# Attention units ordered by query block, with row statistics once for four heads

## The chip, the cores and the metric

One Trainium2 chip, one of its cores. The metric is the device time of one execution in microseconds (us). An execution has one launch; the time is that of the core from start to end. The engines are named TensorE (PE in the profile, its weight loads PEld), VectorE (DVE), ScalarE (ACT), GpSimd (POOL) and SyncE (SP).

## The reference

The whole model runs over 512 tokens of width 1024: two layers, each a feed-forward network, a mixer of four kinds of attention and another feed-forward network, and then a third block with a state-space part, a recurrent part and a last feed-forward network. The change is in the mixer's attention, which is computed in each of the two layers. Cut to what matters:

```python
Q_BLOCK, HEADS, HEAD_DIM = 128, 4, 64

def masked_softmax(s, mask):
    s = jnp.where(mask, s, NEG_INF)
    e = jnp.where(mask, jnp.exp(s - jnp.max(s, -1, keepdims=True)), 0.0)
    return e / jnp.maximum(jnp.sum(e, -1, keepdims=True), 1e-30)

# first mixer: per query block, causal, scale 96 ** -0.5
p = masked_softmax(s.astype(jnp.float32) * scale, k_pos[None, :] <= q_pos[:, None])
# second mixer: 31 compressed keys, selected blocks, window; three gated outputs
o = g[:, :, 0] * o_cmp + g[:, :, 1] * o_slc + g[:, :, 2] * o_win
# third mixer: an index score picks 128 keys for each query
_, idx = lax.top_k(score, n_top)
p = masked_softmax(s, (idx <= q_pos[None, :, None])[:, None])
```

With 512 tokens the selection of the second mixer takes all its blocks, and its window all past keys, so both are causal attention over all keys so far.

## The kernel before

Everything stays in the core's on-chip memory; weights stream in by DMA. The work is written in phases with a barrier between them. Each phase gives every engine its own instruction list, and semaphores order them. In each layer the mixer has the phases projections, preparation, `mixer_attention`, `mixer_stick_breaking` and output. The change is nearly all in `mixer_attention`.

`mixer_attention` first computes the index scores: 24 tiles of products with 32 rows, a ReLU on ScalarE (L1219) and a weighted sum on VectorE (L1343). The scores of the first three units are issued ahead of it. I call this the index stretch. Then it goes through 80 units. A unit is one head, one block b of 128 queries and one branch: 16 units of the first mixer, 48 of the second (compressed keys, selected, window for every head and block), 16 of the third. A unit is 128, 256, 384 or 512 keys wide by its block, a compressed one 31. The order is head by head, block within head, so that wide and narrow units take turns.

For unit u TensorE runs this loop: scores of unit u + 3 (L1163 to L1167, up to three products and one product of the identity with the mask), two dummy products of 512 columns that only keep it active (`keep_clock`, L373), the transposes of unit u's exponentials (L1178), and the values of unit u - 1 (L1189). ScalarE computes the exponentials with their row sum (L1228) of unit u + 1 and copies the transposed ones of unit u (L1238). VectorE reduces unit u + 2 to its row maximum (L1283), turns it into a bias (L1290), and finishes unit u - 1: clamp (L1296, compressed only), reciprocal (L1301), gate (L1306), product into `mix_y` (L1319 or L1323). Between them it has a round of the search for each query's 128 largest index scores: a MAX8 (L1262) and a value load and replacement (L1269). There are 48 rounds, one in each of the first 48 units: 16 over 256 columns, 16 over 384, 16 over 512. In its first eight units it also splits operands into a high and a low part (L1327).

```python
for u in range(n):
    if u + 3 < n:
        scores(u + 3)
    transposes(u)
    if u >= 1:
        values(u - 1)
```

A unit's scores lie in one of four banks, the transposes in banks 6 and 7, the values in banks 4 and 5.

Of the kernel before, what the change touches and what calls it, by code (L numbers as in the profile page):

```python
# [7 lines left out]
F32 = mybir.dt.float32  # L8
F32R = mybir.dt.float32r
BF16 = mybir.dt.bfloat16  # L10
ALU = mybir.AluOpType
# [43 lines left out]
CONST_NAMES = ["ident", "negd", "negs", "cmpm", "negl", "strict", "ntri", "nones", "ones", "sw64", "sw32", "triu"]  # L55
# [27 lines left out]
def constants():  # L83
# [6 lines left out]
    c["negs"] = (k >= q) * NEG  # L90
# [7 lines left out]
    for b in range(QB):  # L98
        m[:, b * NCMP:(b + 1) * NCMP] = (n[None, :] * 16 + 31 > (i + b * P)[:, None]) * NEG
    c["cmpm"] = m  # L100
    c["triu"] = (k <= q) * 1.0
    c["negl"] = (k > q) * NEG
# [130 lines left out]
class Core:  # L233


    def __init__(self, nc, ctx, dram, outT):
# [14 lines left out]
        self.kb = {name: self.kb_all[:, n * P:(n + 1) * P] for n, name in enumerate(CONST_NAMES[:N_BF16])}  # L251

# [116 lines left out]
def keep_clock(c, pe, bank, n):  # L369


    for _ in range(n):
        pe.matmul(c.ps[:, bank], c.kb["ident"], c.kb_all[:, 0:SEQ], start=True, stop=True, skip_group_check=True)  # L373


def setup_phase(c, following):

    nc, d = c.nc, c.dram
    with ExitStack() as ctx:
        ph = Phase(c, ctx, "setup", "x_in consts_in kb_done ones_done", following=following)  # L380
        with nc.Block() as block:
# [14 lines left out]
            @block.scalar  # L396
            def _(act):
                for u in range(2):
                    ph.split_hi(act, ph.next, 0, u, D)
                act.wait_ge(ph["consts_in"], 16)  # L400
                act.activation(c.kb_all[:], c.consts[:, 0:N_BF16 * P], ACT.Copy).then_inc(ph["kb_done"], 1)
# [392 lines left out]
class Mixer:  # L794


    def __init__(self, c):
# [18 lines left out]
        self.split = {t: (hi[t], self.hr[:, t], self.h[:, t]) for t in (IDXQ, IDXQ + 1, IDXK, NSAQ, NSAQ + 1, KSLC, KWIN, DSAQ, DSAQ + 1, DSAK)}  # L816
        self.split["kc"] = (self.kch[:], self.kcl[:], self.kc[:])
# [85 lines left out]
def mixer_preparation(c, m, l):  # L903
# [19 lines left out]
    with ExitStack() as ctx:  # L923
        ph = Phase(c, ctx, "prep", "w_in c1_in c2_in swap_done cos_done sin_done rope_done sq_done sum_done std_done rstd_done "
                   "lat_done uq_done qm_done uk_done km_done kpe_done uv_done vm_done win_done hid_done gelu_done kv_done cmp_done pad_done ukv_in")
        with nc.Block() as block:
# [58 lines left out]
            def _(act):  # L985
# [5 lines left out]
                for h in range(HEADS):  # L991
                    act.wait_ge(ph["uq_done"], h + 1)
                    act.activation(m.qm[:, h], c.ps[0:96, 4 + h], ACT.Copy).then_inc(ph["qm_done"], 1)
# [65 lines left out]
def attention_units(m, c):  # L1059

    units = []

    def part(tile, h, at):

        return [x[64 * (h % 2):64 * (h % 2) + 64, at] for x in m.split[tile][:2]]

    for h in range(HEADS):  # L1070
        for b in range(QB):
            units.append(dict(q=[m.qm[:, h, b * P:(b + 1) * P]], k=[m.km[:, h, 0:(b + 1) * P]], mask=c.kb["negd"], at=b * P, width=(b + 1) * P,
                              scale=96 ** -0.5, v=[m.vm[:, j, h * HD:(h + 1) * HD] for j in range(b + 1)], gate=None, mixer=0, h=h, b=b,
                              first=True, clamp=False))
    for h in range(HEADS):
        for b in range(QB):
            q = part(NSAQ + h // 2, h, slice(b * P, (b + 1) * P))
            units.append(dict(q=q, k=part("kc", h, slice(0, NCMP + 1)), mask=c.kb["cmpm"][:, b * NCMP:(b + 1) * NCMP], at=0, width=NCMP, scale=HD ** -0.5,
                              v=[m.vc[:]], gate=m.tok[:, b, GATE + h:GATE + h + 1], mixer=1, h=h, b=b, first=True, clamp=True))
            for br, (kt, vt) in enumerate(((KSLC, VSLC), (KWIN, VWIN))):  # L1080
                g = GATE + (br + 1) * HEADS + h
                units.append(dict(q=q, k=part(kt, h, slice(0, (b + 1) * P)), mask=c.kb["negd"], at=b * P, width=(b + 1) * P,
                                  scale=HD ** -0.5, v=[m.tok[:, j, vt:vt + HD] for j in range(b + 1)], gate=m.tok[:, b, g:g + 1],
                                  mixer=1, h=h, b=b, first=False, clamp=False))
    return units


def dsa_units(m, c, allowed):
    units = []
    for h in range(HEADS):  # L1090
        lo = 64 * (h % 2)
        for b in range(QB):
            mask = c.kb["negd"] if b == 0 else allowed[b]
            units.append(dict(q=[x[lo:lo + 64, b * P:(b + 1) * P] for x in m.split[DSAQ + h // 2][:2]],
                              k=[x[lo:lo + 64, 0:(b + 1) * P] for x in m.split[DSAK][:2]], mask=mask, at=0,
                              width=(b + 1) * P, scale=HD ** -0.5, v=[m.tok[:, j, DSAV:DSAV + HD] for j in range(b + 1)], gate=None,
                              mixer=2, h=h, b=b, first=True, clamp=False))
    return units


def mixer_attention(c, m, l):
# [17 lines left out]
    stat = c.at("att_stat", [P, 4, 8], F32, off)  # L1119
    top8 = c.at("idx_top", [P, 8], F32, off + 128)[:]  # L1120
    units = attention_units(m, c)
    n_dsa = len(units)
    units += dsa_units(m, c, allowed)
# [7 lines left out]
    with ExitStack() as ctx:  # L1131
        ph = Phase(c, ctx, "att", "hi_done lo_done rel_done relu_done acc_done scores_done max_done nmax_done exp_done sum_done rinv_done scale_done t_done "
                   "pt_done pv_done y_done top_done took_done choice_done")
        with nc.Block() as block:
            @block.tensor
            def _(pe):
# [13 lines left out]
                def scores(u):  # L1150
# [16 lines left out]
                    pe.matmul(s[:, x["at"]:x["at"] + mw], c.kb["ident"], x["mask"], start=False, stop=True).then_inc(ph["scores_done"], 1)  # L1167

                def transposes(u):
# [4 lines left out]
                    keep_clock(c, pe, 6 + u % 2, 2)  # L1174
# [6 lines left out]
                def values(u):  # L1181
                    x = units[u]
                    pe.wait_ge(ph["pt_done"], u + 1)
                    if u >= 2:

                        pe.wait_ge(ph["y_done"], u - 1)
                    w = min(P, x["width"])
                    for j, v in enumerate(x["v"]):
                        mm = pe.matmul(c.ps[:, 4 + u % 2, 0:HD], pt[0:w, u % 2, j * P:(j + 1) * P], v, start=j == 0, stop=j == len(x["v"]) - 1)  # L1189
# [18 lines left out]
            def _(act):  # L1208
                def hi(i):
                    act.activation(splits[i][0], splits[i][2], ACT.Copy).then_inc(ph["hi_done"], 1)  # L1210
# [11 lines left out]
                def exponentials(u):  # L1222
                    x = units[u]
                    act.wait_ge(ph["nmax_done"], u + 1)
                    if u >= 3:

                        act.wait_ge(ph["t_done"], u - 2)
                    act.activation(p[:, u % 3, 0:x["width"]], c.ps[:, u % 4, 0:x["width"]], ACT.Exp, scale=x["scale"],  # L1228
                                   bias=stat[:, u % 4, 1:2], accum_out=stat[:, u % 4, 2:3]).then_inc(ph["exp_done"], 1)
# [19 lines left out]
            def _(dve):  # L1249
# [29 lines left out]
                def maximum(u):  # L1279
                    x = units[u]  # L1280
                    s = u % 4
                    dve.wait_ge(ph["scores_done"], u + 1)
                    dve.reduce_max(stat[:, s, 0:1], c.ps[:, u % 4, 0:x["width"]], AXX).then_inc(ph["max_done"], 1)  # L1283

                def bias(u):
                    x = units[u]
                    s = u % 4
                    dve.wait_ge(ph["max_done"], u + 1)

                    dve.tensor_scalar(stat[:, s, 1:2], stat[:, s, 0:1], -x["scale"], 1e27, ALU.mult, ALU.min).then_inc(ph["nmax_done"], 1)  # L1290

                def clamp_sum(u):
                    dve.wait_ge(ph["exp_done"], u + 1)
                    if units[u]["clamp"]:
                        total = stat[:, u % 4, 2:3]
                        dve.tensor_scalar(total, total, 1e-30, None, ALU.max).then_inc(ph["sum_done"], 1)  # L1296

# [1138 lines left out]
```

## Time and profile before

| what | value |
|---|---|
| time, median of 3 runs | 3755.67 us (3751.5 to 3755.68) |
| time of the profiled execution | 3753.07 us |
| its span, first to last instruction | 3751.3 us |
| mean granted clock of TensorE | 0.964 of 2.4 GHz |
| TensorE busy | 3530.4 us, 94% |
| VectorE busy | 1705.3 us, 45% |
| ScalarE busy | 1437.4 us, 38% |
| units of `mixer_attention`, first layer | 614 to 769 us |
| units of `mixer_attention`, second layer | 1859 to 2015 us |

The busy time of an engine is the time in which it has an instruction in flight. Instructions overlap, so a duration is longer than the step from one start to the next; it is the steps that add up. In the timelines, instructions of one line that follow each other are merged, with their count; float32 products count twice there. The granted clock is 1.00 at 2.4 GHz and 0.50 at 1.2 GHz.

### The profile page before, as it was taken

The page shows a single profiled execution, that of the slowest core. Times are in us where ns is not written, and L with a number is a line of the kernel's source. Part 1 is how long each engine was busy: PE and PEld are TensorE (multiplying, and loading weights), DVE is VectorE, ACT ScalarE, POOL GpSimd, SP SyncE. Part 2 cuts the span into 40 slices and gives each one's busy share as a digit, 9 for nine tenths or more (in the row PEclk, how much of TensorE's full clock was granted, in tenths as well). Part 3 has the DMA queues.
Part 4 walks back from the last instruction along what each step waited for, and adds up shares of the span by engine and source line. Part 5 has one row for each costly group of instructions (what it writes and reads, how often), then busy time and mean ns, then how long its engine had stood idle before and what let it go on. Part 6 is the DMA issues. An engine that isn't in the chain of part 4 may idle for free. (4 is left out here: it accounts for less than half of the span.)

```text
span 3751.3 us, 44207 instructions
## 1 busy us (share of the span) xinstructions
PE 3530.4 (94%) x16234; PEld 2792.0 (74%) x16234; DVE 1705.3 (45%) x2929; ACT 1437.4 (38%) x2361; POOL 126.2 (3%) x92
## 2 busy tenths in 40 slices
PE   7999989989999999999899899989999899889998
PEld 5888766767887788778477688766777677768886
DVE  3333438735333433342783533345566536443332
ACT  3332424454332333232445533234554527433321
POOL 0001011001001000100200100000000000000000
PEclk9999998989999999999799999998999999999999
DMA  3332210002232223322000133311112122222231
GB/s 132 95 108 89 99 64 1 1 12 80 96 105 95 68 95 99 101 95 73 19 1 1 64 99 95 104 55 63 63 63 69 46 88 96 85 78 90 95 105 69
DMA packets 75671, 277.43 MB, mean 74 GB/s; under 512 B 12288, under 2 KB 13824, under 8 KB 74752
## 3 DMA queue, kind: packets, MB, share of 16 engines
q1 hardware_dynamic: 75520, 275.45, 22.4%
q8 instruction: 91, 1.49, 0.2%
q14 instruction: 60, 0.49, 0.0%
HBM read 273.32 MB, written 2.10 MB: 73 GB/s over the span
## 5 line engine op out<-in xcount | busy, mean ns | idle before, releaser
L318 DVE TENSOR_TENSOR wlo<-raw,whi 128x1024 fp32r<-128x1024 f32 (+2 forms) x464 | 610.0, 1315 | 1034.2 <-ACT whi L314 1034.2
L346 PE MATMUL ps<-xh,whi 128*128 128x512 f32 x2384 | 932.4, 391 | 16.3 <-DVE xl L2384 6.3
L347 PE MATMUL ps<-xl,whi 128*128 128x512 f32 x2384 | 929.0, 390 | 0.0
L348 PE MATMUL ps<-xh,wlo 128*128 128x512 f32 x2384 | 928.7, 390 | 0.0
L314 ACT ACTIVATE whi<-raw 128x1024 fp32r<-128x1024 f32 (+2 forms) x464 | 515.7, 1111 | 621.9 <-PE ps L348 613.7
L346 PEld LDWEIGHTS ps<-xh,whi 128*128 128x128 f32 x2384 | 448.4, 188 | 115.9 <-issue 22.2
L347 PEld LDWEIGHTS ps<-xl,whi 128*128 128x128 f32 x2384 | 448.6, 188 | 93.8 <-issue 0.7
L348 PEld LDWEIGHTS ps<-xh,wlo 128*128 128x128 f32 x2384 | 448.5, 188 | 93.4
L346 PE MATMUL ps<-ffn_hh,whi 128*128 128x512 f32 x880 | 346.9, 394 | 11.1 <-DVE ffn_hl L750 11.1
L347 PE MATMUL ps<-ffn_hl,whi 128*128 128x512 f32 x880 | 345.3, 392 | 0.0
L348 PE MATMUL ps<-ffn_hh,wlo 128*128 128x512 f32 x880 | 345.0, 392 | 0.0
L705 ACT ACTIVATE ffn_hh<-ffn_gate 128x512 f32 (+1 forms) x110 | 69.6, 633 | 511.8 <-DVE ffn_gate L748 511.8
L748 DVE TENSOR_TENSOR ffn_gate<-ffn_gate,ps 128x512 f32<-128x512 f32 x110 | 75.6, 688 | 282.2 <-PE ps L348 282.2
L346 PEld LDWEIGHTS ps<-ffn_hh,whi 128*128 128x128 f32 x880 | 166.9, 190 | 49.1 <-DVE ffn_hl L750 13.2
L347 PEld LDWEIGHTS ps<-ffn_hl,whi 128*128 128x128 f32 x880 | 166.4, 189 | 35.5 <-issue 1.0
L348 PEld LDWEIGHTS ps<-ffn_hh,wlo 128*128 128x128 f32 x880 | 166.8, 190 | 34.9
L1799 PE MATMUL ps<-xh,whi 128*128 128x512 f32 x384 | 160.0, 417 | 17.7 <-PEq L297 17.7
L701 ACT ACTIVATE ffn_gate<-ps 128x512 f32<-128x512 f32 x110 | 65.8, 598 | 256.3 <-PE ps L348 254.3
L1800 PE MATMUL ps<-xl,whi 128*128 128x512 f32 x384 | 152.9, 398 | 0.0
L1801 PE MATMUL ps<-xh,wlo 128*128 128x512 f32 x384 | 152.9, 398 | 0.0
L508 POOL TENSOR_TENSOR x<-x,mean_rest 128x512 f32<-128x512 f32 x48 | 77.3, 1646 | 1869.8 <-ACT mean_rest L472 1869.8
L750 DVE TENSOR_TENSOR ffn_hl<-ffn_gate,ffn_hh 128x512 f32 (+1 forms) x110 | 76.2, 693 | 98.9 <-ACT ffn_hh L705 98.9
(375 smaller groups left out, 4452.8 us busy)
## 6 DMA issues: line engine op xcount, KB each, us to landing
raw<-in_ffn_up SPq DMA_DIRECT2D x216, 512.0 KB, 3.5
raw<-in_ffn_down SPq DMA_DIRECT2D x80, 704.0 KB, 4.0
raw<-in_ssm_in SPq DMA_DIRECT2D x44, 512.0 KB, 3.5
raw<-in_mix_in SPq DMA_DIRECT2D x40, 512.0 KB, 3.5
raw<-in_lru_in SPq DMA_DIRECT2D x20, 512.0 KB, 3.6
raw<-in_mix_out SPq DMA_DIRECT2D x16, 512.0 KB, 3.6
raw<-in_ssm_out SPq DMA_DIRECT2D x16, 512.0 KB, 3.5
raw<-in_lru_out SPq DMA_DIRECT2D x8, 640.0 KB, 3.9
```

Source lines behind the costliest of these rows:

```text
L314: act.activation(self.core.whi[:, u % HALF, 0:width], self.core.raw[:, u, 0:width], ACT.Copy).then_inc(sems["hi_done"], 1)
L318: dve.tensor_tensor(self.core.wlo[:, u % HALF, 0:width], self.core.raw[:, u, 0:width], self.core.whi[:, u % HALF, 0:width].bitcast(F32), A ...
L346: pe.matmul(out, c.whi[:, h, w], xh[:, k0 + k], start=first and k == 0, stop=False)
L347: pe.matmul(out, c.whi[:, h, w], xl[:, k0 + k], start=False, stop=False)
L348: mm = pe.matmul(out, c.wlo[:, h, w], xh[:, k0 + k], start=False, stop=last and k == nk - 1)
L508: pool.tensor_tensor(c.x[:, t], c.x[:, t], c.dneg[:], ALU.add).then_inc(ph["xc_done"], 1)
L705: act.activation(hh[:, p], gate[:, u // 2], ACT.Copy).then_inc(ph["hh_done"], 1)
L748: dve.tensor_tensor(gate[:, u // 2], gate[:, u // 2], c.ps[:, u], ALU.mult).then_inc(ph["prod_done"], 1)
L750: dve.tensor_tensor(hl[:, p], gate[:, u // 2], hh[:, p].bitcast(F32), ALU.subtract).then_inc(ph["hl_done"], 1)
L1799: pe.matmul(out, c.whi[:, h, w], c.xh[:, t], start=t == 0, stop=False)
L1800: pe.matmul(out, c.whi[:, h, w], c.xl[:, t], start=False, stop=False)
L1801: mm = pe.matmul(out, c.wlo[:, h, w], c.xh[:, t], start=False, stop=t == DT - 1)
```

## The change

- **Order.** Units are grouped: for each mixer, block and branch, the four heads follow each other. First mixer blocks 0 to 3; second mixer, per block, compressed, selected and window; third mixer blocks 0 to 3. So four units of one width stand in a row, and the second mixer starts with sixteen short units (compressed, selected 128, window 128, compressed).
- **Sign.** Queries are scaled by the negative of their scale where they are copied or split anyway, and the mask is added through a negated identity. The row statistic is then the least score, and it is the bias of the exponential as it stands; the scaling instruction (L1290) falls away. For compressed units one more column, a small masked value, bounds the least score.
- **Once for four heads.** The row sums of four heads lie beside each other. Reciprocal, clamp, gate and the product into `mix_y` come once for a group, over 4 or 256 columns, in the second unit behind it. A group that adds to `mix_y` has a product into a buffer and an addition. The values of four heads share one bank.
- **Dummies.** Units narrower than 256 get three dummy products, all others two.
- The constants for the masks of two other phases change their sign too.

The core of the diff:

```diff
+    for b in range(QB):
+        own, past = slice(b * P, (b + 1) * P), slice(0, (b + 1) * P)
+        q = lambda h: part(NSAQ + h // 2, h, own)
+        group(1, b, q, lambda h: part("kc", h, slice(0, NCMP + 1)), c.kb["cmpm"][:, b * (NCMP + 1):(b + 1) * (NCMP + 1)], 0, NCMP,
+              lambda h: [m.vc[:]], gate=m.tok[:, b, GATE:GATE + HEADS], least=NCMP + 1)
+        for br, (kt, vt) in enumerate(((KSLC, VSLC), (KWIN, VWIN))):
+            g = GATE + (br + 1) * HEADS
+            group(1, b, q, lambda h: part(kt, h, past), c.kb["negd"], b * P, (b + 1) * P,
+                  lambda h: [m.tok[:, j, vt:vt + HD] for j in range(b + 1)], gate=m.tok[:, b, g:g + HEADS], first=False)
...
-                    pe.matmul(s[:, x["at"]:x["at"] + mw], c.kb["ident"], x["mask"], start=False, stop=True).then_inc(ph["scores_done"], 1)
+                    pe.matmul(s[:, x["at"]:x["at"] + mw], c.kb["nident"], x["mask"], start=False, stop=True).then_inc(ph["scores_done"], 1)
...
-                    keep_clock(c, pe, 6 + u % 2, 2)
+                    keep_clock(c, pe, 6 + u % 2, 3 if x["width"] < 2 * P else 2)
...
-                    if u >= 2:
-
-                        pe.wait_ge(ph["y_done"], u - 1)
+                    if u % HEADS == 0 and u >= 2 * HEADS:
+
+                        pe.wait_ge(ph["y_done"], u // HEADS - 1)
...
-                    act.wait_ge(ph["nmax_done"], u + 1)
+                    act.wait_ge(ph["least_done"], u + 1)
+                    if u % HEADS == 0 and u >= 2 * HEADS:
+
+                        act.wait_ge(ph["rinv_done"], u // HEADS - 1)
...
+                def minimum(u):
                     x = units[u]
                     dve.wait_ge(ph["scores_done"], u + 1)
+                    if u >= 4:
+
+                        dve.wait_ge(ph["exp_done"], u - 3)
+                    dve.tensor_reduce(least[:, u % 4:u % 4 + 1], c.ps[:, u % 4, 0:x["least"]], AXX, ALU.min).then_inc(ph["least_done"], 1)
+
+                def finish(n):
+
+                    g = groups[n]
+                    tot, inv = total[:, n % 2], inverse[:, n % 2]
+                    dve.wait_ge(ph["exp_done"], HEADS * (n + 1))
+                    if g["clamp"]:
+                        dve.tensor_scalar(tot, tot, 1e-30, None, ALU.max).then_inc(ph["sum_done"], 1)
+                        dve.wait_ge(ph["sum_done"], sum(y["clamp"] for y in groups[:n + 1]))
+                    dve.reciprocal(inv, tot).then_inc(ph["rinv_done"], 1)
+                    dve.wait_ge(ph["rinv_done"], n + 1)
+                    if g["gate"] is not None:
+                        dve.tensor_tensor(inv, inv, g["gate"], ALU.mult).then_inc(ph["scale_done"], 1)
+                        dve.wait_ge(ph["scale_done"], sum(y["gate"] is not None for y in groups[:n + 1]))
+                    dve.wait_ge(ph["pv_done"], HEADS * (n + 1))
...
+                    if g["first"]:
+                        dve.tensor_tensor(out.rearrange(heads, d=HD), src, factor, ALU.mult).then_inc(ph["y_done"], 1)
                     else:
+                        dve.tensor_tensor(part[:].rearrange(heads, d=HD), src, factor, ALU.mult).then_inc(ph["part_done"], 1)
+                        dve.wait_ge(ph["part_done"], sum(not y["first"] for y in groups[:n + 1]))
+                        dve.wait_ge(ph["y_done"], n)
+                        dve.tensor_tensor(out, out, part[:], ALU.add).then_inc(ph["y_done"], 1)
...
                 for u in range(n):
                     if u + 2 < n:
+                        minimum(u + 2)
                     largest()
+                    if u % HEADS == 1 and u > HEADS:
+                        finish(u // HEADS - 1)
                     take()
                     if u < len(splits) - n_index:
                         lo(n_index + u)
+                    allow()
+                finish(len(groups) - 1)
```

## Rows read from the trace of the kernel before

**Rows 1.** Windows: stretch, length, busy (PE, PEld, DVE, ACT, POOL), clock, DMA.
```profile
593.00:612.80 19.80, 19.09 (x81) 16.75 (x81) 14.63 (x30) 12.22 (x27) 0.00 (x0) 0.52 0.00 1
614.00:618.00 4.00, 4.00 (x16) 2.29 (x14) 3.87 (x15) 2.94 (x11) 0.00 (x0) 0.52 0.00 0
645.04:667.16 22.12, 22.12 (x146) 16.31 (x146) 21.31 (x100) 10.48 (x36) 0.00 (x0) 1.00 0.00 1
667.16:689.46 22.30, 22.30 (x146) 16.25 (x146) 21.76 (x94) 9.68 (x34) 0.00 (x0) 1.00 0.01 1
689.46:713.97 24.51, 23.31 (x146) 16.20 (x146) 22.83 (x99) 10.03 (x38) 0.00 (x0) 1.00 0.00 1
1935.14:1959.66 24.52, 23.32 (x147) 16.20 (x147) 22.83 (x99) 10.04 (x38) 0.00 (x0) 1.00 0.00 1
```

**Rows 2.** Timeline of TensorE, third mixer: start, duration (us), instruction.
```profile
744.59 0.50 PE L1163 MATMUL ps<-index_hi,mix_h_split 64*128 64x512 f32 x1
...
745.70 0.59 PE L373 MATMUL ps<-consts_bf 128*128 128x512 bf16 x2
746.13 0.27 PE L1178 MATMUL ps<-consts_sb,att_p 128*128 128x128 f32 x1
746.24 1.00 PE L1189 MATMUL ps<-mix_tok_sb,att_pt 128*128 128x64 f32 x8
747.18 0.33 PE L1163 MATMUL ps<-index_hi,mix_h_split 64*128 64x128 f32 x1
```

**Rows 3.** Timeline of TensorE, short units of the second mixer.
```profile
669.67 0.27 PE L1178 MATMUL ps<-consts_sb,att_p 128*128 128x128 f32 x1
669.88 0.43 PE L1189 MATMUL ps<-cmp_v,att_pt 31*128 31x64 f32 x2
670.24 0.38 PE L1163 MATMUL ps<-mix_h_split 64*128 64x256 f32 x1
...
670.85 0.59 PE L373 MATMUL ps<-consts_bf 128*128 128x512 bf16 x2
671.29 0.27 PE L1178 MATMUL ps<-consts_sb,att_p 128*128 128x128 f32 x1
671.39 0.33 PE L1189 MATMUL ps<-mix_tok_sb,att_pt 128*128 128x64 f32 x2
671.66 0.28 PE L1163 MATMUL ps<-cmp_k_hi,mix_h_split 64*128 64x32 f32 x1
...
672.13 0.59 PE L373 MATMUL ps<-consts_bf 128*128 128x512 bf16 x2
```

**Rows 4.** Timeline of VectorE, one unit beside a search round of 512 columns.
```profile
682.89 0.68 DVE L1283 TENSOR_REDUCE att_stat<-ps 128x1 f32<-128x512 f32 x1
683.49 0.68 DVE L1262 MAX8 idx_top<-idx_score 128x8 f32<-128x512 f32 x1
...
684.21 0.09 DVE L1269 MATCH_VALUE_LOAD idx_score<-idx_top,idx_score 128x8 f32 x1
684.28 0.68 DVE L1269 MATCH_REPLACE8 idx_score<-idx_top,idx_score 128x512 f32<-128x512 f32 x1
684.88 0.15 DVE L1306 TENSOR_TENSOR att_stat<-att_stat,mix_tok_sb 128x1 f32<-128x1 f32 x1
...
685.26 0.68 DVE L1283 TENSOR_REDUCE att_stat<-ps 128x1 f32<-128x512 f32 x1
```

**Rows 5.** Statistics by tile: count, then shortest/median/longest duration in ns.
```profile
L1283 DVE TENSOR_REDUCE att_stat<-ps x160: 178/414/686, 595.7 to 2010.1; 128x1 f32<-128x128 f32 x32, 128x1 f32<-128x256 f32 x32, 128x1 f32<-128x384 f32 x32, 128x1 f32<-128x512 f32 x32
...
L1262 DVE MAX8 idx_top<-idx_score x96: 415/551/686, 614.9 to 1951.9; 128x8 f32<-128x256 f32 x32, 128x8 f32<-128x384 f32 x32, 128x8 f32<-128x512 f32 x32
```

**Rows 6.** Timeline of TensorE, scores ahead of the index stretch.
```profile
593.11 0.46 PE L1163 MATMUL ps<-mla_k,mla_q 96*128 96x128 f32 x2 [1.18 <-PEq L297]
...
593.47 0.65 PE L1163 MATMUL ps<-mla_k,mla_q 96*128 96x256 f32 x2
...
594.02 1.59 PE L1163 MATMUL ps<-mla_k,mla_q 96*128 96x384 f32 x2
```

More of the change, by code:

```diff
@@ L1056, in mixer_preparation, with attention_groups @@
         ph.end()
-def attention_units(m, c):
-    units = []
+def attention_groups(m, c, allowed):
+    groups = []
     def part(tile, h, at):
         return [x[64 * (h % 2):64 * (h % 2) + 64, at] for x in m.split[tile][:2]]
[L1070 to L1085, printed above, removed]
@@ L1088, in dsa_units, with group @@
[L1088 to L1098, printed above, removed]
+    def group(mixer, b, q, k, mask, at, width, v, gate=None, first=True, least=None):
+        units = [dict(q=q(h), k=k(h), mask=mask, at=at, width=width, least=least or width, v=v(h), h=h) for h in range(HEADS)]
+        groups.append(dict(units=units, mixer=mixer, b=b, gate=gate, first=first, clamp=least is not None))
@@ L1101, in mixer_attention @@
+    for b in range(QB):
+        own, past = slice(b * P, (b + 1) * P), slice(0, (b + 1) * P)
+        group(2, b, lambda h: part(DSAQ + h // 2, h, own), lambda h: [x[64 * (h % 2):64 * (h % 2) + 64, past] for x in m.split[DSAK][:2]],
+              c.kb["negd"] if b == 0 else allowed[b], 0, (b + 1) * P, lambda h: [m.tok[:, j, DSAV:DSAV + HD] for j in range(b + 1)])
+    return groups
 def mixer_attention(c, m, l):
@@ L1117, in mixer_attention @@
         off += sizes[b] * 2
[L1119 to L1123, printed above, removed]
+    least = c.at("att_least", [P, 8], F32, off)
+    total = c.at("att_total", [P, 2, HEADS], F32, off + 32)
+    inverse = c.at("att_inverse", [P, 2, HEADS], F32, off + 64)
+    top8 = c.at("idx_top", [P, 8], F32, off + 96)[:]
+    part = c.at("att_part", [P, HEADS * HD], F32, off + 128)
+    groups = attention_groups(m, c, allowed)
+    units = [x for g in groups for x in g["units"]]
+    n_dsa = len(units) - QB * HEADS
     n = len(units)
@@ L1292, in clamp_sum @@
[L1292 to L1296, printed above, removed]
-                def invert_sum(u):
-                    if units[u]["clamp"]:
-                        dve.wait_ge(ph["sum_done"], sum(y["clamp"] for y in units[:u + 1]))
-                    dve.reciprocal(stat[:, u % 4, 3:4], stat[:, u % 4, 2:3]).then_inc(ph["rinv_done"], 1)
@@ L1331, in _ @@
                 for u in range(2):
-                    maximum(u)
-                    bias(u)
+                    minimum(u)
                 for i, (b, h) in enumerate(rels):
```

91 lines of the change are left out of this document (34 added, 57 removed).

## The prediction

> **What bounds the kernel now.** I read the page's slices first, to see how busy TensorE is and at what clock, then the windows view over the attention phase, then the timelines of TensorE and VectorE inside it. The change touches one phase that runs twice, once in each layer: 80 units of attention (one head, one block of 128 queries, one branch). The windows of [rows 1] begin where TensorE starts the dummy products of units 16, 28, 40 and 52, so each holds twelve units with the same mixture of shapes. The reader is to see the lengths: 22.12, 22.30, 24.51 us. TensorE is filled in the first two: its timeline [rows 2] shows one iteration, the dummies at 745.70, the transpose at 746.13, the values at 746.24, the next scores at 747.18, each starting where the one before has streamed, with no wait between. So the phase goes at TensorE's pace, except in units 40 to 51, where 24.51 - 22.12 = 2.4 us are lost. There VectorE runs search rounds over 512 columns and needs 2.37 us for a 512 wide unit, 0.5 less for the narrowest [rows 4, 5], while TensorE has light units. The 0.18 us of the window before makes the loss 2.6 us a layer. The second layer has the same 24.52 us [rows 1]. The granted clock is 1.00 (2.4 GHz) in all these windows, and 0.52 in the index stretch and in the first four microseconds of the units.
>
> TensorE's prices, start to start: two dummies 0.43 us, so 0.215 each; one transposed block 0.11; values of four blocks 0.94 [rows 2]; in a unit 128 wide, values 0.27; in a compressed one 0.36, behind a transpose that takes 0.21 and not 0.11; its scores 0.47 [rows 3].
>
> **Part by part.**
>
> *The third dummy.* It stands in every unit narrower than 256: in each layer 4 units of the first mixer, 16 compressed, 8 of the two other branches, 4 of the index mixer, 32 in all. 32 x 0.215 = 6.9 us a layer on the engine that sets the pace. It would be free only where TensorE waits for something. Before, it waits in units 40 to 51, by 2.4 us; after, the short units stand elsewhere, so I cover none of it. Bounds: 2.4 us a layer covered, or none. Those in the first four units run at half clock, up to 0.8 us more; they may also bring the clock up sooner, so I take the full-clock price.
>
> *The order.* Scores of units 0 to 2 are computed before the index stretch, where nothing waits for them [rows 6]. Before, they are 128, 256 and 384 wide, after, 128 three times. The first costs 0.36 us, the second 0.55 [rows 6], the third some 0.74 by the same step. So 0.19 + 0.38 = 0.6 us of work moves from a covered place onto the path. The other products are the same in number and shape; the mask product keeps its form with the sign turned, the scaling rides on copies that are there already: nothing.
>
> *VectorE's work.* Removed per unit: the bias, the reciprocal, the gate and the product into y. The row statistics show how little that frees: from the MAX8 at 683.49 to the value load at 684.21 are 0.72 us, 0.68 of them the MAX8 itself [rows 4], and the bias and the reciprocal lie in what is left. Only the gate and the product show, 684.88 to 685.26, 0.38 us. The group's end comes instead, once in four units: reciprocal, gate, a product over 256 columns out of PSUM, for the two branches an addition too, each waiting for the last. The trace has no such product; the nearest row is the reduction over 256 columns, the median 0.41 us [rows 5]. I take 0.19 for each short step and 0.4 for each wide one: 0.6 us for a plain group, 0.9 for a compressed one, 1.2 for the two branches, 0.15, 0.23 and 0.30 a unit; bounds of the wide step 0.3 (0.41 less overlap) and 0.6 (twice a column's price for the broadcast). So a unit of the two branches gets back 0.08 us, not the five instructions' sum.
>
> Is VectorE late after? Search rounds now meet other shapes: 256 columns with the first mixer, 384 with sixteen short units, 512 with 256 wide, compressed and 384 wide units. Round plus replacement is 0.72 + 0.07 + 0.60 = 1.39 us at 512 columns [rows 4] and 0.27 less at 384, two times 0.13 as the medians of the MAX8 step [rows 5]: 1.12. Reductions are 0.10 (32 columns), 0.20, 0.33, 0.47, 0.60 after overlap. Sixteen short units: VectorE about 24.5 us, TensorE 8 x (1.47 + 0.215) + 8 x (1.34 + 0.215) = 25.9, where 1.47 is 0.47 + 0.43 + 0.11 + 0.46 and 1.34 a 128-wide unit likewise (0.53 for its scores). Each further 128 columns add 0.11 transposed, 0.22 for values (0.94 less 0.27, over three) and up to 0.19 for scores, whose 512 columns take 1.11 [rows 2]: 1.75 for 256, 2.25 for 384, 2.8 for 512. Not late. Next, eight units 256 wide and four compressed: VectorE 8 x 2.02 + 4 x 1.72 = 23.0, TensorE about 8 x 1.75 + 4 x 1.69 = 20.8, and the scores of the wider units ahead add 0.4: 21.2. VectorE falls back by 1.8 us, 2.1 with the last round's choice of keys in it. It may: it reduces unit u+2 while TensorE transposes u, so it can be two iterations behind, 2 x 1.7 = 3.4 us, before an exponential is late. After that the 384 and 512 wide units let it catch up. I take the lag as absorbed; the bound is all 2.1 us a layer, or 3.5 with the wide step at 0.6.
>
> Beside this, a rule. Two more instructions, bias and reciprocal, stand between the MAX8 and the value load of [rows 4] and cost 0.04 us beyond the MAX8's own 0.68. The Trainium skill, "VectorE: DVE Perf Modes", section "The DRAIN you can't avoid", says that a next operation doesn't start until the pipe is empty, so that each instruction taken away would give back its whole duration. By that rule VectorE would gain some 0.25 us a unit more and never be late: the sum below would stay at 3765.8 and its upper bound go. The trace doesn't bear it out, so the bound stays.
>
> *The first eight units.* Here VectorE also splits operands, 0.60 us for 512 columns as for the reduction of that width [rows 4]: 0.86 for a round over 256 columns, 0.20 to 0.33 for the reduction, 0.60, so 1.66 to 1.80 us, against 1.25 and 1.6 on TensorE (its 128 and 256 wide units of the first mixer, third dummy in). That is 2.4 us behind over eight units, less the some 1.9 us that TensorE itself loses in four at half clock [rows 1]: within the lead, nothing.
>
> *The waits.* The first exponential of a group waits for the reciprocal of the group but one before, and the first values for that group's product. Both are issued at the latest three units earlier; behind them stand ScalarE's transposed copies and TensorE's next scores, which would be late only if VectorE were behind by three units. The reduction waits for an exponential four units back, which the scores' own wait already covers: nothing. ScalarE is busy 10 of 22 us [rows 1], and no DMA is touched.
>
> *The loss of before.* With no light units of TensorE under the 512-column rounds, the 2.6 us a layer come back.
>
> *The end.* The last group ends with a 256-column product in place of one over 64: some 0.15 us.
>
> **Sum.** Per layer 6.9 + 0.6 + 0.15 - 2.6 = 5.05 us, twice 10.1. Against the profiled execution's own 3753.07 us that is 3763.2. The median shown, 3755.67, stands 2.6 above it, so I forecast 3765.8. Its own range by the bounds above: with 2.4 of the dummies covered 3761, with VectorE late by 2.1 a layer 3770, by 3.5 3773.
>
> **Rivals.**
>
> *Not slower: the gaps around the compressed values close.* TensorE runs all its instructions in a row, so its time can only fall if an instruction gets cheaper. The candidate is the 31-row weight load of the compressed values. It follows a 128-row transpose today and costs 0.10 us ahead of it and 0.09 in itself [rows 3]. With four compressed units in a row it would stand behind a transpose of its own kind in three of four. If all of it went, 32 units x 0.19 = 6.1 us, the time is 3759.7, no change. It decides from 2.6 us, half of the gaps. For it: nothing that the load needs is late, its data lie ready. Against it: the transposes still use 128 rows. 0.24.
> The Trainium skill, "TensorE: Matmul & The Clock Gate", section "Architectural detail: the array is 16× 32×32, not 1× 128×128", says that the queue can pull a weight load ahead of matmuls in flight; by it the gap could close, 3759.7. Behind the 128-row transpose of [rows 3] it stays open.
>
> *VectorE is late in the 512-column rounds.* The group's end is a chain of dependent steps in front of the replacement, and delays it all at once. 3770 to 3773. For it: VectorE was busy 21.76 of 22.30 us before [rows 1]. Against: the lead. 0.16.
>
> *The clock falls in the sixteen short units in a row.* The index stretch shows that TensorE can be busy 19.09 of 19.80 us at 0.52 [rows 1], with products of 32 rows. At half clock a short unit costs about 1.3 us more; 16 units and two layers are 42 us: 3807. Against: three dummies are 0.645 of 1.6 us, and windows with two to a unit hold 1.00. 0.06.
> The Trainium skill, "TensorE: Matmul & The Clock Gate", Part 4 on PE-mode transposes, says that transposes don't count as busy for the clock. The two short iterations of [rows 3] lie in a window granted 1.00 with transposes in it, so no row here refutes the rule or needs it; by it this rival would give the same 3807.
>
> *The short units' dummies are hidden and the loss returns.* TensorE would have to wait there; the sum says it doesn't. Then 2 x (0.75 - 2.6) = -3.7 us, 3752. 0.04.
>
> **How the numbers follow.** Forecast case 0.50; the four rivals 0.24, 0.16, 0.06, 0.04. Within 0.2% (7.5 us, about what a measurement of this kernel can tell from no change) means 3748 to 3763.2. The forecast lies only 2.6 us above that edge, so I give a sixth of its case, 0.08, to no change: slower 0.42 + 0.16 + 0.06 = 0.64, of which 0.02 go to faster for what I haven't seen, 0.62. Of the 0.28 of the two cases that aren't slower, 0.22 stay with no change and 0.06 go to faster, for closed gaps together with a clock that rises sooner: same 0.08 + 0.22 = 0.30, faster 0.06 + 0.02 = 0.08. The range runs from the first rival with some margin, 3757, to the late VectorE with some, 3775.
>
> **What would show it.** In the profile after: 384 dummies over both layers instead of 320; iterations of the short units at about 1.5 to 1.7 us; no stretch of 24.5 us; TensorE without waits for exponentials in units 32 to 47; granted clock 1.00 from about 618 us on; the phase's units 5 us longer in each layer. Wrong it would be if the compressed values start 0.11 us behind their transposes, if TensorE waits for VectorE's least score, or if the clock is below 1.00 between units 16 and 31.

## The result and the profile after

The changed kernel takes 3763.68 us (median of 13, 3756.99 to 3766.95), the kernel before 3752.26 us (13, 3744.48 to 3756.87): ratio 1.0032, 95% interval 1.0023 to 1.0040. It is slower by 11 us, more than 0.2%. The forecast was 3765.8 us.

The first two windows are those of [rows 1], with its columns. The next three begin at the dummies of units 16, 28 and 40, so here each holds the twelve units of the second mixer of one block. The last is all 80 units.

```profile
593.00:612.80 19.80, 18.50 (x82) 16.88 (x82) 14.51 (x29) 12.28 (x28) 0.00 (x0) 0.50 0.00 1
614.00:618.00 4.00, 4.00 (x17) 2.32 (x16) 3.93 (x13) 2.93 (x13) 0.00 (x0) 0.64 0.00 0
645.73:665.65 19.92, 19.92 (x128) 13.77 (x128) 17.35 (x58) 7.11 (x36) 0.00 (x0) 1.00 0.01 1
665.65:686.16 20.51, 20.51 (x136) 14.83 (x136) 19.92 (x56) 8.83 (x37) 0.00 (x0) 1.00 0.00 1
686.16:710.70 24.54, 24.54 (x160) 17.95 (x160) 19.32 (x53) 10.77 (x36) 0.00 (x0) 1.00 0.00 1
613.26:769.97 156.71, 156.71 (x993) 112.70 (x991) 103.45 (x300) 73.09 (x248) 0.00 (x0) 0.99 0.00 1
```

TensorE has an instruction in flight in every microsecond of the units, 156.71 of 156.71, where it had none for 1.2 us of the 24.51 in [rows 1]. The stretch of 24.54 us is no loss: it holds other units than [rows 1] and is full. VectorE's busy time in the units is 103.45 us where it was 121.50 (613 to 770 us before), since the statistics' small instructions are gone.

The waits between 612 and 774 us, first those of the kernel before, then those after (engine, line, what it waited for: us in all, times, longest):

```profile
ACT att_pt L1238 <- PE ps L1178: 52.5, 58, 1.5
ACT att_p L1228 <- DVE att_stat L1290: 26.0, 30, 1.6
...
PEld ps L1189 <- issue: 4.1, 18, 0.6
```
```profile
ACT att_pt L1241 <- PE ps L1177: 83.8, 78, 1.9
DVE att_least L1288 <- PE ps L1166: 41.8, 32, 2.1
...
PEld ps L1189 <- issue: 4.4, 16, 0.3
...
ACT att_p L1231 <- DVE att_least L1288: 0.7, 2, 0.4
```

Before, the exponentials waited 26.0 us for VectorE; now 0.7 us, and VectorE waits 41.8 us for TensorE's scores. So TensorE sets the pace. The wait in front of the values' weight load is as long as it was. The timeline of TensorE over two compressed units in a row answers to [rows 3]:

```profile
648.61 0.27 PE L1177 MATMUL ps<-consts_sb,att_p 128*31 128x128 f32 x1
648.81 0.43 PE L1189 MATMUL ps<-cmp_v,att_pt 31*128 31x64 f32 x2
649.17 0.32 PE L1162 MATMUL ps<-mix_h_split 64*128 64x128 f32 x1
...
649.72 0.81 PE L376 MATMUL ps<-consts_bf 128*128 128x512 bf16 x3
650.37 0.27 PE L1177 MATMUL ps<-consts_sb,att_p 128*31 128x128 f32 x1
650.57 0.43 PE L1189 MATMUL ps<-cmp_v,att_pt 31*128 31x64 f32 x2
650.93 0.32 PE L1162 MATMUL ps<-mix_h_split 64*128 64x128 f32 x1
```

Three dummies take 0.65 us (649.72 to 650.37), 0.217 each; transpose to values is still 0.20 and values to the next scores 0.36, also behind a unit of the same kind. The whole step of such a unit is 1.76 us (648.61 to 650.37), just above the 1.5 to 1.7 us of the forecast's sign. The statistics by line count the dummies, 384 where two to each of the 160 units would be 320:

```profile
L376 PE MATMUL ps<-consts_bf x384: 376/379/634, 613.3 to 2023.3; 128*128 128x512 bf16 x192
```

VectorE's group end of a compressed group beside a 512-column round answers to [rows 4]:

```profile
697.00 0.68 DVE L1265 MAX8 idx_top<-idx_score 128x8 f32<-128x512 f32 x1
697.60 0.15 DVE L1296 TENSOR_SCALAR att_total<-att_total 128x4 f32<-128x4 f32 x1
697.79 0.18 DVE L1298 RECIPROCAL att_inverse<-att_total 128x4 f32<-128x4 f32 x1
698.00 0.17 DVE L1301 TENSOR_TENSOR att_inverse<-att_inverse,mix_tok_sb 128x4 f32<-128x4 f32 x1
698.20 0.42 DVE L1310 TENSOR_TENSOR mix_y<-ps,att_inverse 128x256 f32<-128x256 f32 x1
698.54 0.08 DVE L1272 MATCH_VALUE_LOAD idx_score<-idx_top,idx_score 128x8 f32 x1
```

The end of a clamped group takes 0.94 us (697.60 to 698.54) where 0.9 was estimated: the small steps are 0.19 to 0.21, the wide one 0.34. From the MAX8 to the value load are 1.54 us where [rows 4] have 0.72, so 0.82 more.

**Where the time went.** The table has the length of the phase, from the first ReLU of the index stretch (layer 2: its last) to the first exponential of the stick-breaking part, read from the two tiles' start times, and what lies between the two. The labels are those of the experiments below; all lengths are in us, from the profiled execution:

| kernel | layer 1 | layer 2 | between |
|---|---|---|---|
| before | 176.70 | 161.37 | 1084.3 |
| after | 181.45 | 165.57 | 1087.5 |
| new_two | 175.39 | 159.88 | 1086.0 |
| old_three | 181.98 | 165.35 | 1081.7 |
| old_order_three | 184.67 | 168.40 | 1085.3 |
| new_512_one | 171.87 | 156.42 | 1086.0 |
| new_two_desc | 174.95 | 159.06 | 1083.8 |
| desc_512_one | 171.07 | 155.69 | 1086.6 |
| desc_384_one | 167.80 | 152.28 | 1083.4 |

The phase grew by 4.8 and 4.2 us. That the layers differ comes from the first four units, in part of which the clock is still at 0.50: after, they take 7.45 and 7.07 us at a mean granted clock of 0.76 and 0.80, before 8.03 and 8.21 us. Behind them the two layers of a kernel agree within 0.02 us, before and after.

The 3.2 us between lie in phases whose instructions the change leaves the same in number and shape, and in the index stretch of layer 2, which takes 15.49 us in every kernel of the table. TensorE's clock steps down in parts of this stretch, and in each trace elsewhere. An example, the windows that start 80 us ahead of the second layer's last ReLU, before and after:

```profile
1777.80:1787.80 10.00, 7.84 (x33) 5.71 (x32) 2.29 (x5) 2.53 (x6) 2.12 (x2) 1.00 0.09 22
```
```profile
1785.40:1795.40 10.00, 7.87 (x23) 4.62 (x22) 3.05 (x6) 3.16 (x5) 3.71 (x3) 0.83 0.36 104
```

But the mean granted clock of the whole stretch is 0.97 before, after and in old_three, so this doesn't account for the differences; what does wasn't settled. The column goes from 1081.7 to 1087.5. So the phase lengths are the finer measure of each edit, and differences of 3 us in a total aren't read.

### The profile page after: what moved, and what is told of

It reads as the page before. It is cut to its first block and busy times, and to the rows that moved or that the text cites. A ratio compares the mean times of both kernels' runs of the same rounds, so it can differ in the third digit from the quotient of the medians.

```text
span 3763.6 us, 43662 instructions
## 1 busy us (share of the span) xinstructions
PE 3541.3 (94%) x16298; PEld 2797.1 (74%) x16298; DVE 1669.5 (44%) x2449; ACT 1434.8 (38%) x2362; POOL 126.2 (3%) x92
## 5 line engine op out<-in xcount | busy, mean ns | idle before, releaser
L1241 ACT ACTIVATE att_pt<-ps 31x128 f32<-31x128 f32 (+4 forms) x160 | 64.4, 403 | 166.1 <-PE ps L1177 165.8
```

## The experiments

Each kernel was timed in five rounds beside the kernel before. The first four ran on one chip (before: 3752.78 us), the next four on another (3750.5), the last two on that again (3750.66). The ratios on record aren't always the quotients of the medians; where the two differ by more than 0.1%, both are given.

**new_two: the change with two dummies everywhere**

```diff
-                    keep_clock(c, pe, 6 + u % 2, 3 if x["width"] < 2 * P else 2)
+                    keep_clock(c, pe, 6 + u % 2, 2)
```

> The kernel after, with two dummy products in every unit; the short units lose their third. My account (TensorE sets the pace, each dummy costs its 0.215 us): 64 x 0.215 = 13.8 us off the kernel after, less some 1.3 us a layer for VectorE, which then falls 4.7 us behind where its lead is 3.4: about 3753, a ratio of 1.000 to before. Rival, the clock falls in the sixteen short units in a row: granted clock below 1.00 there and up to 42 us more, 3795. Rival, the third dummy was hidden behind a wait: 3764, as the kernel after.

3752.59 us (3750.7 to 3756.77), ratio 1.0002, 0.9990 to 1.0013. Against the change's own phases the third dummies are 6.1 and 5.7 us; against the kernel before, order and statistics gain 1.3 and 1.5. Without the third dummies VectorE shows: the exponentials wait 21.5 us for it. The wait over the whole phase, and the windows of all units and of units 42 to 45:

```profile
ACT att_p L1231 <- DVE att_least L1288: 21.5, 24, 2.4
```
```profile
613.00:763.64 150.64, 150.43 (x960) 109.39 (x959) 103.05 (x300) 73.31 (x248) 0.00 (x0) 0.99 0.00 1
...
685.61:693.84 8.23, 8.04 (x45) 5.07 (x46) 8.02 (x21) 3.30 (x12) 0.00 (x0) 1.00 0.00 1
```

TensorE's idle time is only 0.21 us, 0.19 of it in the second row. But idle time shows too little, as the steps of unit 44 do, from its dummies to its transposes:

```profile
689.17 0.59 PE L376 MATMUL ps<-consts_bf 128*128 128x512 bf16 x2
689.96 0.55 PE L1177 MATMUL ps<-consts_sb,att_p 128*128 128x128 f32 x3 [0.20 <-ACT att_p L1231]
```

They are 0.79 us where two dummies take 0.43. Compared unit by unit with the change (from the start of a unit's dummies to the next), 29 of the 32 short units of layer 1 are shorter by 0.21 to 0.22, the price of the dummy. Unit 40 is longer by 0.19 in spite of its missing dummy, and unit 44 by 0.41. So VectorE's lag costs some 0.8 us a layer; its lead of two units takes up the rest. In layer 2 the first two units, in which the clock rises, give back 0.4 us less than their two dummies.

**old_three: the kernel before with three dummies in short units** (the same line, the other way round)

> The kernel before, with three dummy products in the units narrower than 256, nothing else changed. My account: 32 a layer at 0.215 us are 6.9 us, of which the units that wait for VectorE in the 512-column rounds hide at most 2.4: 9 to 13.8 us over two layers, a ratio of 1.0024 to 1.0037. Rival, the slowdown comes from the new order or the grouped statistics and not from the dummy: 0 to 3 us.

3757.84 us (3755.41 to 3761.76), ratio 1.0010, 0.9992 to 1.0028. The phases grew by 5.3 and 4.0 us, 9.3 in all, at the lower end of what was expected; the total by 5, since the stretch between was 2.6 us shorter and the one behind the second phase 2.1. Without the first two units, in which the clock rises, the growth is 4.5 us in both layers. That fits dummies partly hidden in the units of [rows 1] where TensorE waits: 6.9 less 2.4 is 4.5 a layer.

**old_order: the new order with the old statistics, two dummies**

```diff
-    for h in range(HEADS):
-        for b in range(QB):
+    for b in range(QB):
+        for h in range(HEADS):
...
-            for br, (kt, vt) in enumerate(((KSLC, VSLC), (KWIN, VWIN))):
+        for br, (kt, vt) in enumerate(((KSLC, VSLC), (KWIN, VWIN))):
+            for h in range(HEADS):
```

> The kernel before with its units in the new order (four heads in a row), its statistics per unit and its two dummies. My account: VectorE's price per unit stays 1.66 to 2.11 us while sixteen short units stand in a row, then 256 wide and compressed ones under 512 columns: it falls about 9 us behind TensorE, some 3 are absorbed, so 6 a layer are lost in place of 2.6, and 0.6 for the scores ahead: 8 us slower, 1.002. If order is free because VectorE is never the bound: 1 us slower. If the clock falls in the short units: below 1.00 there and 20 us or more.

3791.04 us (3757.43 to 3823.6), ratio 1.0065, 1.0040 to 1.0090 (quotient of the medians 1.0102). The eleven executions fall into two kinds: three at 3757 to 3760 us with a mean granted clock of 0.966 to 0.967, eight at 3787 to 3824 with 0.946 to 0.958. The first are where the expectation's main account lies, the second are its case of a falling clock. The profiled one is of the second kind (3811.66 us). Its windows of units 34 to 37, 38 to 41 and 42 to 44, then the stretch from the fall to the rise of the clock and what follows it:

```profile
672.26:680.61 8.35, 7.75 (x49) 5.27 (x50) 8.21 (x33) 3.28 (x13) 0.00 (x0) 1.00 0.00 1
680.61:690.21 9.60, 9.11 (x47) 5.55 (x46) 9.42 (x42) 3.33 (x16) 0.00 (x0) 0.82 0.00 1
690.21:700.00 9.79, 9.79 (x29) 5.61 (x29) 8.50 (x32) 3.09 (x11) 0.00 (x0) 0.50 0.01 2
...
686.85:748.29 61.44, 61.44 (x210) 41.35 (x209) 28.27 (x125) 15.64 (x52) 0.00 (x0) 0.50 0.00 1
748.29:795.00 46.71, 46.71 (x309) 35.70 (x310) 20.73 (x91) 21.14 (x63) 0.00 (x0) 1.00 0.01 1
```

VectorE is late (8.21 of 8.35 us busy) and TensorE stands still for 0.60 and 0.49 us. Then its clock falls to 1.2 GHz in unit 40, and it stays there for 61.44 us although TensorE is busy in all of them. It rises in unit 57, 512 keys wide, and holds to the end of the units. new_two has the same order and the same dummies and never fell in 11 executions, so it is the statistics per unit that make the difference. That they do so by making VectorE late fits the trace (in the first two windows the exponentials wait 12.7 us for it), but new_short_one shows that a fall needs no late VectorE.

**new_wide_one: the change, two dummies in short units, one in all others**

```diff
-                    keep_clock(c, pe, 6 + u % 2, 3 if x["width"] < 2 * P else 2)
+                    keep_clock(c, pe, 6 + u % 2, 2 if x["width"] < 2 * P else 1)
```

> The kernel after with one dummy fewer in every unit: two in the short ones, one in the others. My account: 160 x 0.215 = 34 us off the kernel after, less what VectorE then holds back, 2 to 4 us a layer: 3733 to 3738, a ratio of about 0.995, if the clock stays at 1.00. Rival, the dummies in the wide units keep the clock up: granted clock below 1.00 in stretches and a time of 3770 or more.

3812.97 us (3809.74 to 3830.93), ratio 1.0174, 1.0156 to 1.0193 (quotient of the medians 1.0160). The rival was right. The windows of units 32 to 36 (with the end of 31), of units 37 to 40, from the fall of the clock to its rise, and from there to the end of the units:

```profile
665.00:673.82 8.82, 8.82 (x61) 6.83 (x60) 8.58 (x24) 4.06 (x14) 0.00 (x0) 1.00 0.00 1
673.82:681.75 7.93, 7.47 (x46) 5.01 (x46) 7.69 (x22) 3.46 (x15) 0.00 (x0) 0.98 0.00 0
...
681.47:773.62 92.15, 92.15 (x335) 67.79 (x334) 31.70 (x84) 24.40 (x79) 0.00 (x0) 0.50 0.00 1
773.62:797.50 23.88, 23.88 (x158) 18.46 (x156) 7.55 (x17) 12.60 (x38) 0.00 (x0) 1.00 0.00 1
```

The exponentials wait 8.6 us for VectorE in the first two windows. Gaps of TensorE of 0.46 us in one window stand ahead of 92 us at 1.2 GHz with TensorE busy throughout. The clock falls at the end of unit 40 and rises in unit 66, 128 keys wide and with two dummies; the units of 512 keys with one dummy didn't bring it back. Units of 256, 384 and 512 keys all have one dummy here, so this run doesn't say which of them lack it, nor whether they or VectorE's lag bring the fall.

**old_order_three: old_order with the third dummy in short units**

> The kernel before in the new order, statistics per unit, and three dummies in the short units. In the same order with two dummies the clock fell in most executions (median 3791). Theory: the clock falls where TensorE has few products for its time, under the late VectorE; the third dummy fills that idle time at little cost and keeps the clock at 1.00: 3757 to 3764, and no execution above 3770. Rival, the third dummy doesn't decide, the statistics per unit make VectorE so late that the clock falls all the same: 3780 or more in most executions.

3762.69 us (3757.25 to 3805.07, 12), ratio 1.0036, 1.0013 to 1.0059. One execution of twelve fell in clock (3805 us) where eight of eleven did with two dummies. So in this order the third dummy does keep the clock, for a kernel with the statistics per unit. Its ratio is near that of the full change (1.0032), but the phase lengths tell more: they are 184.67 and 168.40 us against 181.45 and 165.57, so with the third dummy in, statistics once for four heads, with the bias instruction gone, save 3.2 and 2.8 us a layer (2.6 and 2.2 from unit 4 on, where all runs at full clock). And against old_three, which has the old order, the phases are 2.7 and 3.1 us longer: the new order by itself costs about what the grouped statistics give back. This and the third dummy are the parts of the change's 4.8 and 4.2 us.

**new_short_one: the change, one dummy in short units, two in all others**

> The kernel after with one dummy in the short units, two in the others. If the clock stays: 3753 less at most 13.8 us, of which VectorE's lag takes back most, so 3745 to 3751. If the short units need their dummies: the clock falls in units 16 to 31 or 40 to 43, 3780 or more. This is the reach of the third dummy's purpose: with three no fall, with two none in 11 executions, with one I give even odds.

3838.2 us (3834.68 to 3846.4), ratio 1.0236, 1.0222 to 1.0249. Its windows just ahead of the fall (units 17 and 18 and the start of 19), from the fall of the clock to its rise, and from there to the end of the units:

```profile
647.50:650.38 2.88, 2.88 (x19) 1.86 (x19) 2.81 (x11) 1.14 (x6) 0.00 (x0) 1.00 0.00 0
...
650.38:763.02 112.64, 110.88 (x402) 80.29 (x408) 59.98 (x166) 30.26 (x117) 0.00 (x0) 0.50 0.00 1
763.02:809.00 45.98, 45.61 (x302) 35.45 (x306) 13.66 (x34) 21.09 (x63) 0.00 (x0) 1.00 0.00 1
```

Here the clock falls in the sixteen short units, at unit 19 (in layer 2 at unit 22), with TensorE busy 2.88 of 2.88 us just ahead of it and no exponential waiting for VectorE between 640 and 656 us. (The busy time short of a stretch's length further on is no idle time: 16 of the 128 dummies' records of each layer are missing in this trace.) The short units 16 to 19 of new_two, with two dummies, are as full and stay at 1.00:

```profile
644.63:651.27 6.64, 6.64 (x44) 4.58 (x44) 5.56 (x18) 2.28 (x12) 0.00 (x0) 1.00 0.00 0
```

So one dummy is too little there, two are enough. The clock rises again only in the units of 512 keys, 57 in layer 1.

**new_512_one: two dummies, one in units 512 wide**

```diff
-                    keep_clock(c, pe, 6 + u % 2, 3 if x["width"] < 2 * P else 2)
+                    keep_clock(c, pe, 6 + u % 2, 1 if x["width"] == SEQ else 2)
```

> The kernel after with two dummies in every unit, but one in the units 512 wide. If the 512 wide units keep the clock up by their own products: 32 x 0.215 = 6.9 us below the version with two everywhere, 3746, a ratio of 0.998. Rival, their transposes and 64-row products count for little and the dummies are needed there too: granted clock below 1.00 in units 56 to 63, 3770 or more.

3744.99 us (3742.16 to 3748.63), ratio 0.9987, 0.9978 to 0.9996. The phases are 3.5 us shorter than those of new_two in each layer; 16 units a layer by 0.215 are 3.44. The clock holds (the window reaches 4 us past the last unit):

```profile
622.00:765.00 143.00, 139.79 (x905) 104.71 (x920) 94.78 (x274) 66.58 (x225) 0.00 (x0) 1.00 0.00 1
```

**new_two_desc: two dummies, the second mixer's blocks in falling order**

```diff
-    for b in range(QB):
+    for b in reversed(range(QB)):
```

> The kernel after with two dummies everywhere and the second mixer's blocks in falling order, so that the search rounds over 384 and 512 columns lie beside units 512 and 384 wide, and most short units come when the rounds are over. My account: the 1.3 us a layer for which TensorE waits for VectorE go, 3750, a ratio of 0.9993, and no wait for an exponential in units 32 to 47. Rival, VectorE's lag never cost anything: 3753. Rival, the clock falls in the short units that now end the second mixer: 3780 or more.

3749.28 us (3745.21 to 3755.35), ratio 0.9996, 0.9981 to 1.0011. The phases gain 0.4 and 0.8 us on new_two, and without their first four units 0.8 in both layers, which is what VectorE's lag costs in new_two. As the expectation had it, no exponential waits for VectorE in units 32 to 47 (675 to 705 us of the trace). The total gains nothing that can be told from no change.

**desc_512_one and desc_384_one: both edits, one dummy in units 512 wide, or 384 and 512 wide**

```diff
-                    keep_clock(c, pe, 6 + u % 2, 1 if x["width"] == SEQ else 2)
+                    keep_clock(c, pe, 6 + u % 2, 1 if x["width"] >= 3 * P else 2)
```

> The changed kernel with two dummy products in short and wide units, the second mixer's blocks of a head group taken in falling order, and one dummy instead of two in the units of 512 columns. Main account: the two edits don't meet, since the one takes dummy columns from TensorE in the widest units and the other only changes which unit follows which. One dummy less in the 512-column units alone gave 3744.99 us beside 3750.5, and the falling order alone 3749.28; so about 3743 us, ratio 0.998, clock 1.00 in all windows of the units. Rival: with the falling order a group's widest units come first in the group of the second mixer, just behind the short units, and a group that starts with one dummy leaves TensorE short of products there: then the clock falls to 0.50 behind unit 16 or 40 and the time is 3780 us or more. Second rival: the falling order brings the wait for the last weights of a group back: 3748 us or more at full clock.

> As the other kernel of this pair, but one dummy in the units of 384 columns too. Each such unit drops one product of 0.215 us; there are 20 units of 384 columns or near it a layer. Main account: units of 384 columns keep TensorE busy enough by themselves (scores, transposes and values fill 1.9 to 2.3 us of the step), the clock stays 1.00, and the time is about 20 x 0.215 x 2 = 8.6 us less where the whole product is uncovered, so about 3735 us. Rival: the clock falls as it did with one dummy in all wide units (3812.97 us, clock 0.50 from unit 44 on): then 3770 us or more, and the windows show from which unit. Third: the units of 384 columns are paced by VectorE or ScalarE once the dummy is gone, and the time is 3742 us as without this edit.

desc_512_one: 3741.95 us (3738.47 to 3746.61), ratio 0.9961, 0.9937 to 0.9986. desc_384_one: 3735.02 us (3730.0 to 3739.78), ratio 0.9945, 0.9924 to 0.9966. The quotients of the medians are 0.9977 and 0.9958; 4 of the 22 executions of the kernel before took 3777 to 3780 us beside these two, and against the median of the others, 3749.0, they are 0.9981 and 0.9963. The second is the fastest kernel of the study, 15.6 us below the kernel before. The expectation spoke of 20 units of 384 columns; there are 16 a layer, and 16 x 0.215 x 2 = 6.9 us is what the totals differ by (6.93). The clock holds through the units, which end at 758 us:

```profile
620.00:764.00 144.00, 139.47 (x908) 105.94 (x925) 99.88 (x286) 71.50 (x236) 0.00 (x0) 0.99 0.00 1
```

## Why the prediction was right

- *The third dummy*, 6.9 us a layer, uncovered: the largest term, and right in the main. Taking it out gives back 6.1 and 5.7 us. Of what is missing, 0.8 us a layer lie in units 40 and 44: there the third dummies do cover a wait, VectorE's lag, which the forecast took as absorbed. The other 0.4 us of layer 2 lie in the first two units, in which the clock rises. Both are within the bound of 2.4.
- *The loss of before comes back, less the scores ahead and the group's end*: 2.6 - 0.6 - 0.15 = 1.85 us a layer were forecast. Before against new_two gives 1.3 and 1.5, with the 0.8 of VectorE's lag in it, so some 2.2 beside full dummies. No run separates the 0.6 and the 0.15. And the cause isn't the one named: the new order alone does not bring the loss back. With per-unit statistics it lengthens the phase by 2.7 and 3.1 us (old_three to old_order_three), and only the grouped statistics take that off again.
- *VectorE*: the end of a clamped group was estimated at 0.9 us and measured at 0.94, its wide step at 0.4 and 0.34 (three short steps of 0.19 and one wide one add up to 0.97, not 0.9). The bias and the reciprocal that fall away were read as 0.04 us; by steps they are 0.12, since the bias of before starts at 684.09, 0.60 us behind its MAX8, and the value load at 684.21. With the third dummy in, the lag is absorbed, as the forecast has it: the exponentials wait 0.7 us. In new_two, with 0.215 us less of TensorE's work in each short unit, the same lag is 21.5 us of waits of ScalarE and some 0.8 us of TensorE's time.
- *The sum*: 5.05 us a layer against 4.8 and 4.2, so 10.1 against 9.0. The total differs by 11.4 in medians and 12.3 in the profiled spans because 3.2 us came in between the phases, which the forecast has nothing of.
- *The reference point*: the median of the runs shown, 3755.67, was 3.4 us above the median of 13. This error and the 3.2 us between the phases nearly cancel, so it is luck that 3765.8 lies only 2.1 us above the measured 3763.68; the mechanism is borne out by the phase lengths.
- *Rival, the gaps around the compressed values close*: refuted. Transpose to values is 0.20 us and values to scores 0.36 with compressed units in a row. Behind the Trainium skill's sentence on pulled-ahead weight loads ("TensorE: Matmul & The Clock Gate", section "Architectural detail: the array is 16× 32×32, not 1× 128×128") it also has to be said that these loads wait 4.4 us in 16 cases for their issue, so the trace shows no pulling ahead at this place.
- *Rival, VectorE late*: refuted for the change. The mechanism is real, though. In old_order it costs 38 us and not 3, because the clock falls with it. In new_wide_one it stands ahead of the fall too, but there the dummies are fewer as well, and which of the two does it isn't shown.
- *Rival, the clock falls in the sixteen short units*: not with three dummies, nor with two; with one it does (new_short_one). The forecast's price for it was 42 us. With one dummy the time rises by 88, since the clock stays down for 112.64 us of layer 1 and 105.81 of layer 2, far beyond the sixteen units.
- *Rival, the dummies hidden*: refuted by new_two, where 29 of the 32 short units of layer 1 are shorter by a whole dummy.

Of the expectations, that for new_wide_one was the clear miss: its main account lets the clock hold, and it falls in every one of five executions. That for old_order put the falling clock last, and it came in eight of eleven; that for old_order_three had no execution above 3770 us, and one took 3805.

## What to carry to other kernels

Work that only keeps the clock up is paid for in full wherever its engine sets the pace, so count it by shape: here the clock holds with one dummy product in units of 512 keys, and of 384 in the falling order, and with two in short ones, and it falls with one in short ones. Units of 256 keys weren't tried alone. Too few cost 60 to 88 us. How many are enough hangs on the rest of the kernel: with statistics per unit two in short units weren't enough in eight of eleven executions. When an order puts like units in a row, ask of each row whether another engine falls behind in it and whether the first then stands still; the average over the mixture no longer holds. Judge an edit by the length of its own phase when the rest of the program varies by as much as the edit is worth.

## What the runs showed of the hardware

- TensorE's clock can fall while TensorE has an instruction in flight all the time: 2.88 of 2.88 us busy just ahead of the fall in new_short_one. Units 16 to 19 of new_two, 6.64 of 6.64 us busy, were granted 1.00, and so were units 42 to 45 with 8.04 of 8.23. Idle time doesn't tell the cases apart; the number of dummies in the short units differs.
- Once down it stays down through full work: 92.15 of 92.15 us busy at 0.50 (new_wide_one), 61.44 of 61.44 (old_order). It rises within the phase, in the units of 512 keys with two dummies (unit 57 in layer 1 of new_short_one and old_order) or, where these have one, in a unit of 128 keys with two (unit 66, new_wide_one). One dummy in the units of 512 keys holds a high clock (new_512_one) but didn't bring back a low one (new_wide_one).
- Idle time in a profile can be too small: an exponential that came late moved the transposes behind the dummies from 0.43 to 0.79 us, and 0.20 of the 0.36 stand as idle.
- The kernel before isn't free of it: 9 of its 79 executions beside the experiments took 3773 to 3780 us, with a mean clock of 0.957 to 0.959 where the others have 0.963 to 0.968. None of the 13 executions of the changed kernel and of the 57 of new_two, new_512_one, new_two_desc, desc_512_one and desc_384_one did, nor of the 11 of old_three, nor of the 13 of the kernel before beside the changed one. None of the nine was profiled, so where the clock fell and why stays open.
- In the same program a fall can come in some executions and not in others (old_order 8 of 11, old_order_three 1 of 12).
